# Retention in a fused two-block layer: the decayed scores multiply the normed inputs first and the value weights after, and the values are not formed

## The reference, cut to what matters

```
h   = modulate(rmsnorm(rows))                  # 512 rows: 256 of x, 256 of the context; width 1024
q, k, v, g, f, ga, gf = split(h @ w_in)        # v: 4 heads x 512 columns
o   = (decay * (q k^T)) @ v                    # per head: 256 queries, 512 keys; decay depends on distance and direction
on  = (o - mean(o)) * rsqrt(var(o) + eps)      # per head, over its 512 columns
r   = (silu(g) * on * gn_w) @ p_ret
y   = (sigmoid(ga) * r + sigmoid(gf) * fourier(f) @ p_four) @ w_out
```

## Time and profile before

| what | us |
|---|---|
| median of 3 runs | 1663.97 (1663.46 to 1664.26) |
| the profiled execution: its own time | 1664.8 |
| its span (first to last instruction) | 1663.0 |
| PE busy in it | 1646.2 (99%) |
| DVE / ACT busy in it | 1179.5 (71%) / 686.6 (41%) |
| `ret_v`, from 1113.76 to 1200.80 | 87.04 |
| scores, Fourier input, gate, second product, up to `ret_proj` at 1326.60 | 125.80 |

### The profile page before, as it was taken

The page is one execution under the profiler, slowest core; times in us unless marked ns, Lnnn a source line. Parts: engine busy times, 40 slices in busy tenths (PEclk is TensorE's granted clock), DMA queues, the critical chain, the costliest instruction groups (busy, mean ns, idle before and its releaser), DMA issues.

```text
span 1663.0 us, 30217 instructions
## 1 busy us (share of the span) xinstructions
PE 1646.2 (99%) x12232; PEld 1476.1 (89%) x12232; DVE 1179.5 (71%) x1809; ACT 686.6 (41%) x892; POOL 23.9 (1%) x41
## 2 busy tenths in 40 slices
PE   9999999999999999999999999999999999999998
PEld 8999888899999899988888888988889999999997
DVE  7777757564878878668787875942356866688886
ACT  5444456334454444422212222422346445454443
POOL 1000000000000000000000000000000000000000
PEclk9999999999999999999999999999999999999999
DMA  7555477223364555344455542323223355445551
GB/s 285 181 181 193 159 283 274 101 79 104 117 236 177 185 192 187 105 149 152 154 210 216 203 153 76 127 102 104 98 77 109 127 183 198 178 156 198 177 188 65
DMA packets 37832, 267.70 MB, mean 161 GB/s; under 512 B 4269, under 2 KB 4525, under 8 KB 5745
## 3 DMA queue, kind: packets, MB, share of 16 engines
q1 hardware_dynamic: 33552, 238.25, 40.1%
q0 software_dynamic: 4192, 28.19, 4.4%
HBM read 265.38 MB, written 1.05 MB: 160 GB/s over the span
## 4 chain that ended last, share of the span: by engine, by line
PE 42%; issue 23%; DVE 1%; ACT 0%; POOL 0%; POOLq 0%; ACTq 0%; DVEq 0%
PE PS L416 9%; PE PS L417 9%; PE PS L422 6%; PE PS L662 3%; PE PS L633 3%; PE PS L826 2%; PE PS L827 2%; PE PS L825 2%; PE PS L781 2%; PE PS L637 1%; PE PS L1334 1%; PE PS L1319 1%; PE PS L520 0%; DVE HS L1910 0%; PE PS L557 0%
## 5 line engine op out<-in xcount | busy, mean ns | idle before, releaser
L410 DVE TENSOR_TENSOR W_LO<-RAW,W_HI 128x2048 fp32r<-128x2048 f32 x210 | 475.9, 2267 | 153.7 <-ACT W_HI L398 153.1
L398 ACT ACTIVATE W_HI<-RAW 128x2048 fp32r<-128x2048 f32 x208 | 396.7, 1910 | 335.1 <-PE PS L422 142.0
L633 PE MATMUL PS<-HS,W_HI 128*128 128x512 f32 x984 | 246.5, 392 | 0.7 <-DVE W_LO L410 0.7
L416 PE MATMUL PS<-HS,W_HI 128*128 128x512 f32 (+1 forms) x664 | 228.6, 349 | 1.4 <-ACT G L1620 0.8
L417 PE MATMUL PS<-HS,W_LO 128*128 128x512 f32 (+1 forms) x664 | 225.3, 344 | 0.0
L416 PE MATMUL PS<-HID_HI,W_HI 128*128 128x256 f32 (+1 forms) x720 | 221.3, 308 | 2.2 <-DVE XC L1999 1.9
L417 PE MATMUL PS<-HID_HI,W_LO 128*128 128x256 f32 (+1 forms) x720 | 220.1, 306 | 0.0
L662 PE MATMUL PS<-HID_LO,W_HI 128*128 128x256 f32 (+1 forms) x688 | 210.2, 308 | 0.0
L633 PEld LDWEIGHTS PS<-HS,W_HI 128*128 128x128 f32 x984 | 177.0, 189 | 32.6 <-DVE W_LO L410 0.9
L422 PE MATMUL PS<-HS,W_HI 128*128 128x512 f32 (+1 forms) x584 | 205.8, 352 | 0.0
L1999 DVE SCALAR_TENSOR_TENSOR XC<-PS,GATE,XC 128x256 f32<-128x256 f32 x248 | 107.6, 478 | 67.8 <-PE PS L662 67.6
(11 more groups left out here) (420 smaller groups left out, 2328.4 us busy)
## 6 DMA issues: line engine op xcount, KB each, us to landing
RAW<-stream SPq DMA_DIRECT2D x225, 1024.0 KB, 4.8
LATE<-stream POOLq DMA_DIRECT2D x24, 1024.0 KB, 5.1
XC<-xin SPq DMA_DIRECT2D x2, 512.0 KB, 4.7
XC<-xin POOLq DMA_DIRECT2D x1, 1024.0 KB, 6.6
out<-NT SPq DMA_DIRECT2D x4, 256.0 KB, 2.4
CON<-consts POOLq DMA_DIRECT2D x1, 616.0 KB, 6.6
LW<-lora POOLq DMA_DIRECT2D x1, 512.0 KB, 6.8
DFT<-dft POOLq DMA_DIRECT2D x1, 266.0 KB, 3.0
```

Source lines behind the costliest of these rows:

```text
L398: nc.scalar.activation(W_HI[s % RING][:], RAW[PLACE[u]][:], ACT.Copy).then_inc(hi_done, 1)
L410: last = nc.vector.tensor_tensor(W_LO[s % RING][:, o], RAW[PLACE[u]][:, o], W_HI[s % RING][:, o].bitcast(F32), ALU.subtract)
L416: nc.tensor.matmul(acc, w_hi, x_hi, start=first, stop=False)
L633: nc.tensor.matmul(BK8[2 * (t % 2) + w][:].rearrange("p (a n) -> p a n", a=2), W_HI[sl][:, c:c + P], HS[:, :, 0, k], start=(k == 0), stop= ...
```

## The change

Instead of V = H Wv for all 512 rows, and then P V for each head, the kernel after forms (P H) Wv for each head. H is needed with its rows on the partitions, so HS is first turned: `turn_rows` multiplies 64 blocks of 128x128 (32 of the high part, 32 of the low) with an identity in fp32r and collects four at a time in a PSUM bank; ACT copies the high ones to HT, DVE the low ones. `ret_scores(h)` is the loop's product as before. The decayed scores of all four heads are made first and kept in RO; then, head by head, they are split into PT_HI (`probs_hi`, ACT, a copy of 128x1024) and PT_LO (`probs_lo`, DVE, a subtraction). `ret_rows(h)` makes P H in 8 tiles of 128x256, each 4 steps x 3 passes, which ACT (`rows_hi`) and DVE (`rows_lo`) split into PH_HI and PH_LO; `ret_values(h)` multiplies with the value weights, now stationary, in 4 tiles of 8 steps x 3 passes of 256 columns, and `values_out(h)` (ACT) copies these to RO. The gate's units are set between them, with the passes of a tile in the order of `three`. Mean, variance and normalisation of a head (`sum_rows`, `centre`, `sum_squares`, `normalise` on DVE, `centred`, `root_var` on ACT) follow while the next head is on PE; the operations in them are those of before. The value weights come as ordinary tiles, in an order of units that fits. `exps(h)` on ACT holds the five exponentials of before, `fx_out(q)` the two copies to FX, `silu_out(j)` two activations of gate tiles.

In DVE's program the chain of logarithms stays where it was, behind the splits that follow the keys; what stood ahead of it there (8 splits) is now one.

```diff
--- before.py
+++ after.py
-_phase("ret_v", [1, 4] * 4)
 _phase("four_in", [1, 2] * 2)
-_phase("ret_g", [2] * 8)
+_phase("ret_ga", [2] * 2)
+for _h in range(RH):
+    _phase(f"ret_v{_h}", [2] * 2)
+    _phase(f"ret_g{_h}", [2])
+_phase("ret_gb", [2] * 2)
...
+GATE_UNITS = [PHASE["ret_ga"], PHASE["ret_ga"] + 1, *(PHASE[f"ret_g{h}"] for h in range(RH)), PHASE["ret_gb"], PHASE["ret_gb"] + 1]
...
+        def part_at(h, m):
+            return 8 + (KT + 1) * h + m + 2
...
-        DFT_BANK = (6, 2, 3, 0, 1, 7, 6, 2)
+        DFT_BANK = (0, 1, 7, 2, 3, 7, 2, 3)
+        PH_BANK = (7, 0, 1)
+        HT_BANK = (6, 7, 2, 3)
...
-            pe.wait_ge(S("rq_out"), 8)
-            for n in range(8):
-                if n == 2:
-                    pe.wait_ge(S("rk_out"), 8)
-                rows("ret_v", 4, [(0, 0), (0, P), (1, 0), (1, P)], [4, 5, 6, 7, 0, 1, 2, 3], "rv_out", only=n)
...
+            def turn_rows():
+                pe.wait_ge(S("rq_out"), 8)
+                n = 0
+                for tt in range(4):
+                    for dh in range(2):
+                        for part in range(2):
+                            if n >= 4:
+                                pe.wait_ge(S("part_lo" if part else "part_hi"), n // 2 - 1)
+                            for j in range(4):
+                                k = 4 * dh + j
+                                last = nc.tensor.matmul(BK8[HT_BANK[n % 4]][:, j * P:(j + 1) * P], HS[:, part, tt // 2, k, tt % 2 * P:(tt % 2 + 1) * P],
+                                                        IDR[:], start=True, stop=True)
+                            last.then_inc(S("ht"), 1)
+                            n += 1
...
+            def ret_gate(j):
+                s = GATE_UNITS[j]
+                wait_unit(s)
+                if j == 0:
+                    pe.wait_ge(S("fx_out"), 4)
+                sl = s % RING
+                for w in range(2):
+                    if j >= 1:
+                        pe.wait_ge(S("rg_out"), 2 * j + w - 1)
+                    for k in range(KT):
+                        c = (w * KT + k) * P
+                        last = three(BK8[4 + w][:, 0:ROWS], W_HI[sl][:, c:c + P], W_LO[sl][:, c:c + P], xh(k), xl(k), k == 0, k == KT - 1)
+                    last.then_inc(psum_ready, 1)
...
+            def ret_rows(h):
+                if h == 0:
+                    pe.wait_ge(S("pt_out"), RH)
+                pe.wait_ge(S("part_hi"), part_at(h, -1))
+                pe.wait_ge(S("part_lo"), part_at(h, -1))
+                for m in range(KT):
+                    n = KT * h + m
+                    if n >= 3:
+                        pe.wait_ge(S("part_lo"), part_at((n - 3) // KT, (n - 3) % KT))
...
-                    for i in range(4):
-                        for kt in range(4):
-                            last = nc.tensor.matmul(BK8[2 + i // 2][:, (i % 2) * ROWS:(i % 2 + 1) * ROWS],
-                                                    RV[:, kt, h * RDV + i * P:h * RDV + (i + 1) * P], PT[:, kt],
-                                                    start=(kt == 0), stop=(kt == 3))
-                    last.then_inc(S("pv_done"), 1)
...
+                        last = three(BK8[PH_BANK[n % 3]][:, 0:ROWS], HT[:, 0, kt, m * P:(m + 1) * P], HT[:, 1, kt, m * P:(m + 1) * P],
+                                     PT_HI[:, kt], PT_LO[:, kt], kt == 0, kt == 3)
+                    last.then_inc(S("ph"), 1)
+                    if h and m == 1:
+                        ret_mean(h - 1)
+                    if h and m == 5:
+                        ret_var(h - 1)
+            def ret_values(h):
+                pe.wait_ge(S("part_lo"), part_at(h, KT - 1))
+                if h:
+                    pe.wait_ge(S("ro_out"), h)
+                for i in range(4):
+                    s, w = PHASE[f"ret_v{h}"] + i // 2, i % 2
+                    if w == 0:
+                        wait_unit(s)
+                    sl = s % RING
+                    for k in range(KT):
+                        c = (w * KT + k) * P
+                        last = three(BK8[2 + i // 2][:, w * ROWS:(w + 1) * ROWS], W_HI[sl][:, c:c + P], W_LO[sl][:, c:c + P],
+                                     PH_HI[:, k], PH_LO[:, k], k == 0, k == KT - 1)
+                    last.then_inc(psum_ready, 1)
+            rows("four_in", 2, [(0, 0), (0, P)], [4, 5], "fx_out", only=0)
+            pe.wait_ge(S("rk_out"), 8)
+            pe.wait_ge(S("rk_x"), 8)
+            turn_rows()
+            ret_scores(0)
+            for n in range(1, 4):
+                if n == 1:
+                    pe.wait_ge(S("part_lo"), 8)
+                    pe.wait_ge(S("part_hi"), 8)
+                rows("four_in", 2, [(0, 0), (0, P)], [4, 5], "fx_out", only=n)
+                ret_scores(n)
+            ret_gate(0)
+            for h in range(RH):
+                ret_rows(h)
+                ret_gate(h + 1)
+                ret_values(h)
+            ret_gate(RH + 1)
+            ret_mean(RH - 1)
...
                 if q == 5:
-                    pe.wait_ge(S("rvar_rt"), RH)
-                if q >= 6:
-                    pe.wait_ge(S("zz_out"), q - 5)
+                    ret_var(RH - 1)
+                if q >= 5:
...
-            s0 = PHASE["ret_v"]
-            for q in range(4):
-                split_hi(act, s0 + 2 * q + 2)
-                split_hi(act, s0 + 2 * q + 3)
-                for r in range(4):
-                    act.wait_ge(psum_ready, MARK0[s0 + 2 * q + 1] + r + 1)
-                    A(RV[:, r, 512 * q:512 * (q + 1)], BK8[[4, 5, 6, 7, 0, 1, 2, 3][(4 * q + r) % 8]], ACT.Copy).then_inc(S("rv_out"), 1)
...
+            f0 = PHASE["four_in"]
+            split_hi(act, f0 + 2)
+            for n in range(8):
+                act.wait_ge(S("ht"), 2 * n + 1)
+                A(HT[:, 0, n // 2, n % 2 * 512:(n % 2 + 1) * 512], BK8[HT_BANK[2 * n % 4]], ACT.Copy).then_inc(S("part_hi"), 1)
+            exps(0)
+            split_hi(act, f0 + 3)
+            exps(1)
+            split_hi(act, f0 + 4)
+            fx_out(0)
+            exps(2)
+            split_hi(act, f0 + 5)
+            exps(3)
+            probs_hi(0)
+            fx_out(1)
+            split_hi(act, GATE_UNITS[0] + 2)
+            silu_out(0)
+            for h in range(RH):
+                for m in range(KT):
+                    rows_hi(h, m)
+                    if h and m == 3:
+                        centred(h - 1)
+                if h:
+                    root_var(h - 1)
+                if h < RH - 1:
+                    probs_hi(h + 1)
+                split_hi(act, GATE_UNITS[h + 1] + 2)
+                silu_out(h + 1)
+                split_hi(act, PHASE[f"ret_v{h}"] + 2)
+                split_hi(act, PHASE[f"ret_v{h}"] + 3)
+                values_out(h)
+            split_hi(act, GATE_UNITS[RH + 1] + 2)
+            silu_out(RH + 1)
...
-            for s in range(PHASE["ret_v"], PHASE["ret_v"] + 8):
-                split_lo(dve, s + 2)
+            split_lo(dve, PHASE["four_in"] + 2)
...
+            for n in range(8):
+                dve.wait_ge(S("ht"), 2 * n + 2)
+                V.tensor_copy(HT[:, 1, n // 2, n % 2 * 512:(n % 2 + 1) * 512], BK8[HT_BANK[2 * n % 4 + 1]]).then_inc(S("part_lo"), 1)
...
             decay_arg(0)
+            split_lo(dve, PHASE["four_in"] + 3)
+            for h in range(RH):
...
+                if h < 2:
+                    split_lo(dve, PHASE["four_in"] + 4 + h)
+            probs_lo(0)
+            split_lo(dve, GATE_UNITS[0] + 2)
+            for h in range(RH):
+                if h:
+                    sum_rows(h - 1)
+                for m in range(KT):
+                    rows_lo(h, m)
+                    if h and m == 1:
+                        centre(h - 1)
+                    if h and m == 3:
+                        sum_squares(h - 1)
+                if h < RH - 1:
+                    probs_lo(h + 1)
+                split_lo(dve, GATE_UNITS[h + 1] + 2)
+                if h:
+                    normalise(h - 1)
+                if h == 1:
+                    gate_rows(0)
+                    gate_rows(1)
+                if h == 2:
+                    gate_rows(2)
+                if h == 3:
+                    gate_rows(3)
                     r_split(0)
-                    r_split(1)
-                if h >= 1:
-                    dve.wait_ge(S("rvar_rt"), h)
-                    V.reciprocal(RST[:, 1], RST[:, 0]).then_inc(S("rn_rec"), 1)
-                    dve.wait_ge(S("rn_rec"), h)
-                    V.tensor_tensor(ro, ro, RST[:, 1].unsqueeze(1).to_broadcast([P, 4, ROWS]), ALU.mult).then_inc(S("rn_done"), 1)
-                    dve.wait_ge(S("rn_done"), h)
-                if h == RH:
-                    gate_out(2 * h + 1)
-                beside(2 * h + 1)
-                if h < RH:
-                    gate_out(2 * h + 1)
-            dve.wait_ge(S("rg_used"), 12)
+                split_lo(dve, PHASE[f"ret_v{h}"] + 2)
```

(93 more changed lines are left out.)

188 lines of the change are left out of this document (60 added, 128 removed).

## The result

| | median us (lowest to highest) | runs | ratio, 95% interval |
|---|---|---|---|
| before | 1663.79 (1663.17 to 1665.12) | 8 | 1 |
| after | 1668.63 (1667.56 to 1670.33) | 8 | 1.0027 [1.0018, 1.0037] |

A forecast was written before the change was run, and what follows sets the result against it. PE's matmul stream was taken to bound the stage: -15.4 us of work, 15.4 of pauses and 1.7 of later waits gave +1.5, the clock +1.0, so +2.5 on 1663.97: 1666.5 us, range 1659 to 1672.

The forecast's parts named there:

- PE's work in the stage: Matmuls shed and added from the values to `ret_proj`: -87.0 - 27.6 + 92.5 + 7.2 - 0.5 = -15.4 us.
- first pause (HT): After 20 turns PE waits for DVE's first HT copy, behind a split and the logarithms: 5.45 us.
- second (product of head 0): After head 0's scores and a Fourier unit, PE waits for DVE's product `pt_out`, behind a weight split: 3.8 us.
- third (FX): The third Fourier unit waits for ACT's copy to FX, behind exponentials and a split: 3.1 us.
- fourth, fifth: PE waits 0.2 us for a later `pt_out`, then 2.8 us at the first gate unit for the last FX copies.
- tail, two waits: Stage's end: 0.5 us for the last head's row sum behind a weight split, 0.9 us for the variance.
- clock: One clock fall after the longest pause, 1.7 us if all matmuls were clock-bound; +1.0 us added.
- turning in four passes: Rival: turning matmuls cost four passes, 44 exposed turns x 0.1 = 4.5 us more, 1671.0 us; chance 0.06.
- missed waits in the head loop: Rival: the change sheds less than counted, 1 us of waits per head, 1670.5 us; chance 0.07.
- the second stretch: From the end of the first gate unit to the first matmul of `ret_proj`: forecast at 150.4 us.
- PE is fed all the same: Rival: the pauses are half of those counted, 1658.0 us, or 1650.3 with no pause at all; chance 0.13.
- The first rival: Clock falls after the last pause too (1.0 to 1.7 us), and longer after the first: 1670.0 us; chance 0.18.

The follow-up runs named there:

- experiment 8: Experiment 4's kernel with DVE's last sums ahead of a weight split and a gate product, ACT's centring two steps earlier: 1648.31 us, ratio 0.9911.
- experiment 1: After, with the chain of decay logarithms and its two ACT functions moved earlier, into the loop over the keys: 1659.05 us, ratio 0.9964.
- experiment 2: After, with twelve matmuls whose results nobody reads run inside the first pause, the logarithms left in place: 1665.17 us, ratio 1.0005.
- experiment 7: Experiment 4's kernel with every turning matmul made three times, 128 matmuls more: 1664.74 us, ratio 1.0004.
- experiment 4: After, with the edits of experiment 1 and experiment 3 together (logarithms early, new order of splits and FX copies): 1651.12 us, ratio 0.9921.
- experiment 6: After, with the scores of head 0 moved into the first pause, ahead of the sixth group of turns: 1667.52 us, ratio 1.0020.
- experiment 3: After, with ACT's fourth Fourier rounding and FX copies moved earlier and DVE's splits one head later, logarithms in place: 1660.95 us, ratio 0.9983.
- experiment 5: After, with eight f32 matmuls of no use behind the wait of the first pause, ahead of the other 44 turns: 1670.16 us, ratio 1.0037.

## Why the prediction was right, and where it was not

| step | forecast us | in after |
|---|---|---|
| PE's work in the stage | -15.4 | -16.0 (experiment 8) |
| one turn at full clock | 0.1125 | 0.109 to 0.113 (experiments 1, 2 and 7) |
| starts apart in `ret_rows`, `ret_values` | 0.1205 | 0.1200 |
| first pause (HT) | 5.45 | 5.43 |
| second (product of head 0) | 3.8 | 1.52; 3.22 at a full clock (experiment 1) |
| third (FX) | 3.1 | 2.59 |
| fourth, fifth | 0.2, 2.8 | 0, 2.20 |
| tail, two waits | 0.5, 0.9 | 0.54, 0.86 |
| clock | +1.0 | +4.5 (stage of experiment 2) |

**The balance held.** What PE sheds, what it takes on, and that five pauses from program order eat the gain came out step by step, to tenths of a microsecond at most of them. The first price, 27 us of plain f32 matmuls and 87 of values against 92.5 and 7.2, needed no correction by any run. Of the rivals, turning in four passes (0.216 each) and missed waits in the head loop are refuted, the latter by the second stretch, 150.28 against 150.4. "PE is fed all the same" is refuted for after. The number given for it without any of the five pauses, 1650.3, still held 1.7 us of later waits; experiment 4, which has only the two waits of the tail, took 1651.1, and experiment 8, which has none, 1648.3.

**The mis-sized term is the clock.** The step said: one fall after the longest pause, as in the earlier trace rows, 1.7 us if all is bound by the clock, of which I took 1.0. The fall came at that place, and it cost 4.5. Its size was read from a lull that lowered the clock for 3.4 us (twice the 1.7 lost at half speed); here it was low for 17, since what followed the pause was turning, and the turns, twice as slow (9.45 instead of 4.95; nearly in proportion to the clock, so there was no ground to take some of that work as bound by something else), set DVE's casts, hence the tables, hence everything up to the product. Scores of head 0 took 5.01 instead of 3.45. Together 6.1 us. The second wait gave 1.7 of it back, because PE and the chain were late together: it was 1.52 us, where experiment 1 with a full clock has 3.22. The third gave nothing (2.59 and 2.58). That leaves 4.4, and the stages of after and of experiment 2 differ by 4.5. The first rival had this mechanism as its second half, "longer after the first"; that half is what happened, and alone it came to the 3.5 us that the prediction gave for both. Its other half, a fall after the last pause, did not: the clock of the second stretch is 1.00.

**Luck in the total.** The clock term lacked 3.5 us, yet the median lies only 2.3 above the forecast. PE's work came out 0.6 us better than counted, and the pauses, 15.4 us in the ledger, are 5.43 + 3.22 + 2.58 + 2.21 = 13.4 where the clock is full (after for the first, experiment 1 for the others). About 1 us of that difference is a way of counting: from start to start of PE's matmuls the four waits of after are 12.8 us, not 11.7. What remains, some 1.6 us of errors of the other sign, hid nearly half of what the clock term lacked.

The Trainium skill ("TensorE: Matmul & The Clock Gate", "HAM oscillation — how this bites in real kernels") tells of a matmul kernel in which waits of some 3 to 5 us between bursts send the clock down each time. The traces agree for the longer waits (5.43 us in after and 4.02 in experiment 6, both to 0.50); waits of 3.2 us did it in two profiles of three, and those of 2.58 and 2.21 in experiment 1, shorter than the page's, left it at 1.00. The prediction stretched the rule to a fifth pause of 2.8 us and gave it a rival of its own; it was right not to let that decide, but it should have asked what work follows the wait.

**The own times.** From first to last instruction after is 3.2 us longer than before, by medians of runs 4.8. The stage is 4.9 longer; what lies ahead of it was 1.23 shorter in this execution (it began at 1112.53 instead of 1113.76). In the kernel of experiment 6, whose code is the same up to there, it began at 1113.9, so that is scatter between executions, and the clock explains it. At the lull of the earlier trace rows the clock did not fall in the profile of after:

```profile
204.00:206.00 2.00, 2.00 (x19) 1.01 (x22) 1.53 (x4) 0.26 (x1) 0.00 (x0) 1.00 0.00 0
206.00:208.00 2.00, 1.88 (x16) 1.02 (x9) 2.00 (x6) 1.55 (x4) 0.00 (x0) 1.00 0.47 115
```

In the ten profiles of this document it fell there in seven, and the stage began at 1113.3 to 1114.0; it did not in three (after, experiments 3 and 8), and the stage began at 1112.3 to 1112.5. So the same lull lowers the clock in some executions and not in others, and a comparison of whole single profiles carries over a microsecond of it; the length of the stage does not.

**What stays open.** Why a wait of about 3.2 us lowered the clock in experiments 2 and 5 (0.50 behind it) and not in 1, and why in 6 it fell behind only 1.9: the delay from PE's stop to the fall, 1.2 us in after and 4.0 in experiment 5, may be all of it, since a wait of 3.2 lies between the two; that is argued, and no run varies it alone. The lull at 202 us shows that no difference in the kernel is needed for either outcome, so one profile of a kernel does not tell what such a wait does in its other runs. That turning does not restore the clock rests on after, 3 and 6; whether any stream of matmuls as narrow as these behaves so was not tried. In experiment 6 the mean clocks suggest that the fall is missing in some runs; only one was profiled.

## What to carry to other kernels

A stage that PE fills hides whatever DVE and ACT do in it; when a change takes its matmuls out, list what the other engines did under their cover and write their new program as a ledger, since each long step that stands ahead of one that PE needs becomes a wait. Here 15 us of saved matmuls turned into a loss of 5, and two moves of unrelated work (the logarithms, and some splits and copies) turned it into a gain of 13. Price a clock fall by what PE runs behind the pause and by who waits for that, not by the pause: short matmuls kept it low to their end, and filling PE's wait without shortening the other engine's chain only moves the wait.

## What the runs showed of the hardware that was not expected

- A stream of 128-column fp32r matmuls with a weight load each holds a full clock for 21 us (experiment 7), but did not restore a fallen one in 9.4 us (after, experiment 3); 256-column f32 matmuls restored it in 5.4 us (experiment 5), and the scores behind the turns in 3.4 (after).
- In the same pause the clock fell 1.2 us after PE stopped (after) and 4.0 us after (experiment 5).
- At the low clock a turn costs 0.21 instead of 0.11: also the matmuls with a narrow moving side go by the clock.
- A wait of 1.9 us followed by turning lowered the clock (experiment 6); one of 3.2 us followed by scores did not in one profile (experiment 1) and did in two (2 and 5).
- One and the same lull (PE busy 1.23 of 2 us, at 202 us) lowered the clock in seven of ten profiles and left it at 1.00 in three; it moved everything behind it by some 1.3 us.
